# Expert weights fetched two ring slots at a time, on one semaphore per pair of slots

## The reference

```
logits = rmsnorm(x) @ w_router + b_router          # 512 x 32
top 4 of 32 per token, gates = softmax over the 4
for each expert e, for the tokens that chose it:
    gu   = xb @ w_gate_up[e] + b_gate_up[e]        # w_gate_up[e]: 1024 x 2048
    gate = min(gu[:, :1024], 7);  up = clip(gu[:, 1024:], -7, 7)
    act  = (up + 1) * gate * sigmoid(1.702 * gate)
    y    = (act @ w_down[e] + b_down[e]) * token's gate    # w_down[e]: 1024 x 1024
out = rmsnorm(x + sum of the four y of each token)
```

## Time and profile before

| what | value |
|---|---|
| time, median of 3 runs | 1363.3 us (1361.44 to 1363.33) |
| the profiled execution, its own time | 1363.13 us |
| span in its profile | 1361.4 us |
| TensorE busy, share of the span | 1264.2 us, 93% |
| expert loop: first matmul on a weight unit, last one | 335.6 and 1334.6 us |
| first load of the refill loop, last one | 367.0 and 1311.3 us |
| bytes moved | 455.66 MB |

### The profile page before, as it was taken

How to read it: one execution, slowest core, us unless ns; L and a number is a source line. 1 busy time by engine, 2 the same in 40 slices (tenths; PEclk the granted TensorE clock), 3 DMA queues, 4 the chain that set the end, 5 groups by cost and what they waited for, 6 DMA issues and landing times.

```text
span 1361.4 us, 52741 instructions
## 1 busy us (share of the span) xinstructions
PE 1264.2 (93%) x21755; PEld 742.5 (55%) x21755; DVE 520.2 (38%) x1710; ACT 288.4 (21%) x500; POOL 162.0 (12%) x257
## 2 busy tenths in 40 slices
PE   8999999973998999999999999999999999998882
PEld 4546555431655656656555655555565556555451
DVE  6553233226333333333333333343333334332238
ACT  4521124041121221121122121112212212211112
POOL 4100320033010010100101010010100101000010
PEclk9999999985999999999999999999999999999896
DMA  7452151237299999999999999999999999999997
GB/s 238 143 194 91 32 197 46 114 148 302 77 417 418 406 418 406 418 397 418 404 405 417 399 417 408 417 406 417 409 418 403 417 398 404 417 417 418 417 421 282
DMA packets 96851, 455.66 MB, mean 335 GB/s; under 512 B 11033, under 2 KB 22986, under 8 KB 63466
## 3 DMA queue, kind: packets, MB, share of 16 engines
q1 hardware_dynamic: 92768, 445.69, 81.5%
q0 software_dynamic: 3888, 8.40, 1.7%
q10 hardware_dynamic: 90, 0.03, 0.0%
HBM read 432.52 MB, written 23.27 MB: 335 GB/s over the span
## 4 chain that ended last, share of the span: by engine, by line
PE 65%; DMA 30%; DVE 3%; issue 2%; SPq 0%; POOL 0%; ACT 0%; DVEq 0%; POOLq 0%; ACTq 0%
PE ps L1696 25%; DMA ring<-in_w_gate_up_dram 18%; PE ps L1717 12%; PE ps L1309 11%; DMA ring<-in_w_down_dram 10%; PE ps L1658 5%; PE ps L1329 4%; PE ps L1376 1%; DMA x_rows_dram<-cat,rowi 1%; PE ps L1689 1%; PE ps L1708 1%; PE ps L1667 1%; PE ps L1369 1%; PE ps L1338 0%; DMA ring<-x_rows_dram 0%
## 5 line engine op out<-in xcount | busy, mean ns | idle before, releaser
L1696 PE MATMUL ps<-ring,cat 128*32 128x256 f32 x9856 | 557.7, 384 | 15.3 <-DMA ring<-in_w_gate_up_dram 15.3
L1696 PEld LDWEIGHTS ps<-ring,cat 128*32 128x32 f32 x9856 | 308.4, 111 | 236.0 <-DMA ring<-in_w_gate_up_dram 20.1
L1717 PE MATMUL ps<-ring,cat 128*32 128x256 f32 x4928 | 281.5, 379 | 3.9 <-DMA ring<-in_w_down_dram 3.0
L1717 PEld LDWEIGHTS ps<-ring,cat 128*32 128x32 f32 x4928 | 146.0, 110 | 110.5 <-DMA ring<-in_w_down_dram 7.5
L1309 PE MATMUL ps<-hbuf,ring 128*128 128x512 f32 x320 | 147.5, 607 | 0.4 <-DVE hbuf L846 0.4
L778 ACT ACTIVATE cat<-cat 128x128 f32<-128x128 f32 x154 | 47.7, 310 | 453.9 <-DVE cat L1239 453.9
L559 POOL DMA_INDIRECT pair_rows_dram<-cat,rowi x75 | 74.7, 996 | 505.1 <-ACT cat L782 505.1
L1221 DVE TENSOR_REDUCE wslot<-ps 128x2 f32<-128x6 f32 x77 | 12.7, 165 | 317.1 <-ACT cat L782 316.6
L782 ACT ACTIVATE cat<-ps,wslot 128x256 f32<-128x256 f32 x77 | 36.5, 474 | 367.7 <-PE ps L1717 363.0
L1658 PE MATMUL ps<-hbuf,cat 128*32 128x256 bf16 x2496 | 108.7, 274 | 3.7 <-DVE cat L1204 3.7
L1239 DVE TENSOR_SCALAR cat<-ps 128x128 f32<-128x128 f32 x154 | 44.9, 292 | 166.7 <-PE ps L1696 165.2
(11 more groups left out here) (308 smaller groups left out, 816.7 us busy)
## 6 DMA issues: line engine op xcount, KB each, us to landing
ring<-in_w_gate_up_dram SPq DMA_DIRECT2D x256, 1024.0 KB
ring<-in_w_down_dram SPq DMA_DIRECT2D x128, 1024.0 KB
ring<-in_w_in_dram SPq DMA_DIRECT2D x10, 1024.0 KB, 6.3
pair_rows_dram<-cat SPq DMA_DIRECT2D x4, 2048.0 KB, 11.0
ring<-pair_rows_dram SPq DMA_DIRECT2D x4, 2048.0 KB, 20.5
ring<-in_w_out_dram SPq DMA_DIRECT2D x1, 4096.0 KB, 12.9
ring<-in_x_dram SPq DMA_DIRECT2D x4, 512.0 KB, 5.4
x_rows_dram<-ring SPq DMA_DIRECT2D x1, 2048.0 KB, 16.9
```

Of the source, the lines that this page charges most:

```text
L1696: last = mm(ps[SLOTS * q:SLOTS * (q + 1), gu_bank(half), 0:2 * P].rearrange("p (s j i) -> p s j i", s=2, j=4), xgT[:, SLOTS * u:SLOTS * (u ...
L1717: last = mm(ps[SLOTS * q:SLOTS * (q + 1), 1, 0:QD], actT[:, c // 4, SLOTS * (c % 4):SLOTS * (c % 4 + 1)], w[:, i, q * QD:(q + 1) * QD], st ...
```

## The change

Units 20 and up are fetched in pairs, one transfer of 2 MB for two neighbouring units in two neighbouring slots. A pair of slots has one semaphore, ten instead of twenty. Units 0 to 19 are still loaded one at a time, so a pair's semaphore reaches 32 when both of its first units are there, and 16 more for each pair after that (`pair_landed`). Each wait for a unit, on TensorE and on SyncE, now waits for the pair that it is in. SyncE's wait for space asks for both slots of the pair.

```diff
-        slot_in = [sem(f"slot_in{i}") for i in range(RING)]
+        slot_in = [sem(f"slot_in{i}") for i in range(RING // 2)]
...
+        def pair_landed(turn):
+            return 32 + 16 * turn
...
             def load_unit(e, u, slot):
-                sp.dma_start(unit_dst(slot, u), unit_src(e, u)).then_inc(slot_in[slot], 16)
+                sp.dma_start(unit_dst(slot, u), unit_src(e, u)).then_inc(slot_in[slot // 2], 16)
+
+            def load_pair(e, u, slot):
+                if u < NGU:
+                    rows = w_gate_up[0, bass.ds(e, 1), u * P:(u + 2) * P, :].rearrange("a (k p) c -> p (a k) c", p=P)
+                else:
+                    rows = w_down[0, bass.ds(e, 1), 2 * (u - NGU) * P:2 * (u + 2 - NGU) * P, :].rearrange(
+                        "a (k p) c -> p (a k) c", p=P)
+                pair = ring[:, slot * UNIT:(slot + 2) * UNIT].rearrange("p (k c) -> p k c", k=rows.shape[1])
+                sp.dma_start(pair, rows).then_inc(slot_in[slot // 2], 16)
...
-                for u in range(NU):
+                for u in range(0, NU, 2):
                     n = NU * e + u + RING
                     if n >= NU * E:
                         continue
                     landed = n - AHEAD
-                    sp.wait_ge(w_used, used + (u + 1))
-                    sp.wait_ge(slot_in[landed % RING], (landed // RING + 1) * 16)
-                    load_unit(following[n // NU - e], n % NU, n % RING)
+                    sp.wait_ge(w_used, used + (u + 2))
+                    sp.wait_ge(slot_in[landed % RING // 2], pair_landed(landed // RING))
+                    load_pair(following[n // NU - e], n % NU, n % RING)
...
                 def landed(u):
                     slot, turn = slot_of(e, u)
-                    pe.wait_ge(slot_in[slot], (turn + 1) * 16)
+                    pe.wait_ge(slot_in[slot // 2], pair_landed(turn))
```

## The result

The changed kernel takes 1380.41 us (median of 4 runs, 1378.75 to 1381.7), the kernel before 1362.37 us beside it. The ratio is 1.0133, with a 95% interval of 1.0115 to 1.0152: 18 us slower. I had forecast 1370.5, range 1360 to 1377. The direction was right, the size less than half.

What follows compares the result with a forecast made beforehand. Prediction took DMA transfers and TensorE as balanced, both full in the expert loop. Loops 7.4 us plus beginning, last slot wait and end gave 8.9; with 6.0 as alternative, the middle, 7.4, made 1370.5 us, range 1360 to 1377.

Steps and rivals of the forecast that it cites:

- What bounds the kernel: Expert loop: DMA transfers and TensorE balanced, both full; a loop closes in 62.67 us and neither has spare time.
- The wait for both landings: TensorE at a landing it waits for: one down unit more, 0.87 us, less what it had in hand.
- The wait for both slots: SyncE's issue after a slot wait: pair issued 0.43 us later, most of it taken as paid.
- rival A: Expert loop: both waits covered, no change; a loop costs 0.16 us, 1365 us with the end; chance 0.20.
- The sum: Loop terms of both waits less savings: 0.67 us a loop, 7.4 over 11 loops, 8.9 with the other places.
- 0.18, saved on packets and instructions: Refill loop: fewer closing packets and about half of SyncE's refill code save 0.18 to 0.2 us a loop.
- 0.19, engines "still at work" at the first landing: First pair's landing after a slot wait: 0.19 us later than 7.78 on average before, taken off each loop's cost.
- The second sum: If a pair lands 7.54 us after a delayed issue, each of 12 places costs 0.24 less: 6.0 us.
- 0.26, "between landing and use of the last unit": TensorE at a loop's last unit: mean 0.26 us in hand after its landing, taken off each loop's cost.
- Rival C (window too shallow): Pair issue too late when engines differ by over 2.5 us: 18 us, 1381; chance 0.08, row pitch included.
- Size, number and row pitch: Pair transfers: size slows nothing, fixed latency is hidden, halved number saves 1.6 us of packets, rows 1 MB apart cost nothing.
- The signs that I had named: Profile after: w_down waits 0.5 to 0.9 us, loops 63.3, last landing some 6 later, rate between slot waits not below 410.

Runs made afterwards that it cites:

- landing_only: Kernel before, single transfers, but TensorE waits for both units of a pair before starting the first; 1371.77 us.
- last_pair_only: Kernel before, but TensorE waits for unit 11 of an expert before starting unit 10, no other pair waited for; 1372.71 us.
- slots_only: Kernel before, single transfers, but SyncE issues both units of a pair of slots only when the second slot is given back; 1363.12 us.
- both_waits: Kernel before, single transfers and semaphores, with SyncE waiting for both slots and TensorE for both units of a pair; 1380.38 us.
- two_places: last_pair_only, plus SyncE issuing into an expert's first slot only when the second is given back too; 1376.83 us.
- three_places: two_places, plus SyncE waiting for the second slot also for the second pair of slots; 18.8 us over the kernel before.
- pairs_ahead6: Changed kernel with three pairs under way instead of two (AHEAD = 6); 1380.23 us.
- window_only: Kernel before, but units issued two at a time once all but two have landed, slots and landings waited for singly; 1366.36 us.
- quads: Changed kernel with four units to a transfer (4 MB), one semaphore for four slots, two transfers under way; 1428.05 us.

## Why the prediction was wrong, point by point

**What bounds the kernel: right.** The loop from the slot wait through 16 units of transfer to TensorE's use of the last one is where all of it came out.

**The wait for both landings: right in place and size.** One down unit of 0.87 us per loop. landing_only puts 0.74 on a loop and last_pair_only shows that no other pair takes part.

**The wait for both slots: right in size, wrong in how it adds.** The third stretch grew from a typical 17.82 to 19.11 us (medians of the 11 loops), about 0.43 + 0.87: both in full. Alone the same wait was free. I read the cover as the work that the slowest engine still has when the pair is issued at last, that is, how long after that issue the unit before it lands:

| kernel | issue to the landing before it (us, median of 12) | loop (mean of 11) |
|---|---|---|
| before | 2.7 | 62.92 |
| slots_only | 2.3 | 62.95 |
| landing_only | 1.3 | 63.66 |
| both_waits | 0.9 | 64.28 |
| after | 1.0 | 64.50 |

The landing wait makes TensorE's part of the loop longer, so slots come back later against the transfers, which had kept pace, and less is left in the queue at the issue. But the queue is only a part of the cover. The loop in four parts, with the third stretch cut where TensorE ends the down units of the first block (means of the 11 loops of one execution each, us):

| part | before | slots_only | landing_only | both_waits | after |
|---|---|---|---|---|---|
| issue of unit 56 to landing of unit 57 | 7.97 | 7.84 | 7.85 | 7.82 | 7.97 |
| to landing of unit 71 | 36.92 | 36.85 | 36.88 | 37.24 | 37.24 |
| to the end of the down units | 1.33 | 1.16 | 2.26 | 2.17 | 2.20 |
| to the issue of unit 80 | 16.70 | 17.10 | 16.67 | 17.05 | 17.08 |
| loop | 62.92 | 62.95 | 63.66 | 64.28 | 64.50 |

In slots_only the later issue (0.40, last part) is regained in three places: 0.17 in TensorE's spare time at the last unit, 0.13 behind the issue and 0.07 in the second part. With the landing wait there (both_waits against landing_only), 0.12 of its 0.38 is regained in the first and third part, and the second part grows by 0.36 instead: the slot wait is paid in full, and more. My rival A had this cover and my forecast had it gone; both treated it as fixed, while it depends on the other wait.

**The sum: the step that failed.** Its line for one loop was 0.43 + 0.87 - 0.26 - 0.19 - 0.18 = 0.67, measured 1.58. The two costs were nearly right; what it took off, and one term that it did not have, were not:

- 0.18, saved on packets and instructions, and the second stretch as a whole: the largest miss. The small instruction queue did shrink from 23 packets to 16, and the main queue by 2912 packets, 182 x 16, one for each engine and transfer. But the second stretch grew by 0.32 where the sum had -0.18: 0.50 us a loop, 5.5 us in 11. The sum had no term for this growth. It isn't the form of the transfer, as both_waits has the same 37.24, and neither wait alone makes it (36.85 and 36.88). It is also most of why the costs don't add. The loops of slots_only and landing_only are 0.03 and 0.74 longer than before, that of both_waits 1.36, and 0.43 of the 0.59 between lie in this stretch. Single loops scatter from 36.0 to 38.0, which leaves some 0.1 of doubt in a mean of 11: 37.07 in two_places and in three_places lie between, and don't tell which slot wait makes it. Which engine loses the time, and why, stays open.
- 0.19, engines "still at work" at the first landing: not regained in the kernel after, 7.97 as before. In both_waits (7.82) and pairs_ahead6 (7.84) most of it was, so this term is uncertain rather than refuted. The second sum, with a pair that lands 7.54 us after a delayed issue, had no support in any of them, and taking the middle of the two made the forecast 1.5 us smaller.
- 0.26, "between landing and use of the last unit": nearly right. A landing that TensorE waits for is followed by its first matmul 0.04 us later for a single unit (landing at 1321.55, matmul at 1321.59) and 0.12 later for a pair. The least time from landing to the end of the down units is 1.11 us for one unit and 2.05 for a pair; so before had 0.22 to spare on average, nearly half of it in a single loop, and the wait for both costs 0.94, not 0.87. The kernel after has 0.15 on top, the one loop at the lower clock. Together the third stretch is 0.22 over the forecast.

**Rival C (window too shallow): near the time, not the reason.** It gave 1381, by luck. A deeper window changed nothing (pairs_ahead6), though the rhythm alone isn't quite free (window_only). **Size, number and row pitch: right.** both_waits without them takes the same time. By the Trainium skill ("DMA: Bandwidth & Descriptors", section "Rules for kernel authors") a transfer should have 1 MiB or more for the most bandwidth, and many small ones should be coalesced. The traces agree that 1 MB is enough: the full slices move 417 to 418 GB/s with 1 MB, and up to 419 with 2 MB and with 4 MB.

**End: right; beginning: too low.** The end cost 1.0 for 0.9, the transfers behind the last slot wait took 169.1 us in both, the beginning cost 1.7 for 0.6.

**The signs that I had named.** TensorE's waits were 1.4 us for the 0.5 to 0.9 foretold, the loops 64.5 for 63.3 (which is also 0.3 below the sum's own 63.6), the last landing 17.5 us later (1339.07 for 1321.55) for some 6. Between slot waits the rate stayed at 410 GB/s or more, as foretold: 414 from 470 to 504 us, 410 from 536 to 566.

No version here beats the kernel before.

## What to carry to other kernels

In a ring, a coarser transfer makes both hand-overs coarser: the producer waits for more free slots, the consumer for more data. Price each at the one place where the chain passes, and add them without discount; a cover that hides one of them alone may be gone once the other is there. Even that sum, 1.30 us a loop, was short of 1.58: where two engines are both full, test the two waits together, not only one by one. And look at the granted clock behind a wait: in quads it made 19 of the 65 us.

## What the runs showed of the hardware that I had not expected

Waits of TensorE of 3.2 to 3.7 us, once a loop in quads, were each followed by a stretch at the lower of its two clock levels (granted clock 0.51 from 506.5 to 510 us), at 1.7 us each. In the changed kernel, with waits of 1.4 us on average, this happened once in the loops, behind one of 2.04 us, and not behind one of 2.09.

Where the landing before came only 1.0 us after the next pair's issue, the 16 DMA engines moved 98 GB/s over the two microseconds; with 2.7 us they moved 268. Yet the slowest engine's landings in the kernel before had no gap (463.11 and 468.15 us, two units apart), so a share of 0.72 over the engines cost no time there.

Half of SyncE's refill instructions took the small instruction queue from 23 packets to 16, a quarter of them to 12 in quads, so that queue carries SyncE's code. There was no gain in time from it that shows: both_waits, with 22 packets, takes as long as the changed kernel.
